# Nine places for expert weights, another order of the overflow passes, and a reordered router in a two-layer mixture-of-experts kernel

## What is computed

```python
def hierarchical_moe(h, w_rg, b_rg, w_re, b_re, w_gate, w_up, w_down):
    # 4 groups of 8 experts; a token takes the best group and its two best experts
    g_logits = t @ w_rg + b_rg
    g_sel = argmax(g_logits); g_p = softmax(g_logits)[g_sel]
    e_prob = softmax((t @ w_re + b_re)[g_sel])
    top_p, top_i = top_k(e_prob, 2)
    gates = g_p * top_p / sum(top_p)
    # for each of the 32 experts, over the tokens that chose it:
    hid = silu(xb @ w_gate[e]) * (xb @ w_up[e])      # hidden width 256
    y = hid @ w_down[e]
    # out[token] = sum of its two experts' y, each times its gate
```

## Time and profile before

| | us |
|---|---|
| median of 3 runs | 2986.21 (2985.51 to 2987.89) |
| the profiled execution, its own time | 2986.71 |
| its span, first to last instruction | 2985.0 |

### The profile page before, as it was taken

The page is one execution under the profiler, slowest core; times in us unless marked ns, Lnnn a source line. Parts: engine busy times, 40 slices in busy tenths (PEclk is TensorE's granted clock), DMA queues, the critical chain, the costliest instruction groups (busy, mean ns, idle before and its releaser), DMA issues.

```text
span 2985.0 us, 31524 instructions
## 1 busy us (share of the span) xinstructions
PE 2913.9 (98%) x12296; PEld 1856.9 (62%) x12296; DVE 1364.1 (46%) x2249; ACT 609.1 (20%) x1039; POOL 922.8 (31%) x729
## 2 busy tenths in 40 slices
PE   9999999999999999999999999999999999999998
PEld 7865464333468754643333588888664445888887
DVE  6733543333436435432444554442574464644442
ACT  2035323000210263230001400001212351300000
POOL 5500031554124110225551154443220102254442
PEclk9999999999999999999999999999999999999999
DMA  5211125999612201249998222222221111222220
GB/s 192 85 71 43 43 92 186 391 388 393 249 71 87 83 29 57 71 155 370 375 379 328 85 85 85 85 95 88 97 80 57 62 52 57 82 88 85 85 99 29
DMA packets 84165, 412.72 MB, mean 138 GB/s; under 512 B 27572, under 2 KB 30048, under 8 KB 37552
## 3 DMA queue, kind: packets, MB, share of 16 engines
q1 hardware_dynamic: 57664, 387.57, 34.2%
q0 software_dynamic: 26352, 23.12, 2.4%
HBM read 513.31 MB, written 31.46 MB: 183 GB/s over the span
## 4 chain that ended last, share of the span: by engine, by line
PE 89%; DVE 4%; DMA 4%; issue 1%; ACT 1%; SPq 0%; POOL 0%; DVEq 0%; ACTq 0%; POOLq 0%
PE PS L1139 38%; PE PS L1071 9%; PE PS L631 8%; PE PS L1093 5%; PE PS L616 4%; PE PS L709 4%; PE PS L589 4%; PE PS L1312 4%; DMA ring<-in_experts_gu 3%; PE PS L864 1%; PE PS L548 1%; PE PS L804 1%; PE PS L921 1%; PE PS L930 1%; PE PS L1379 1%
## 5 line engine op out<-in xcount | busy, mean ns | idle before, releaser
L3167 POOL TENSOR_TENSOR ATT<-ring 128x512 f32<-128x512 f32 (+1 forms) x97 | 126.3, 1302 | 1178.9 <-PE PS L1139 624.6
L1139 PE MATMUL PS<-G,ATT 128*128 128x256 f32 x1344 | 317.8, 379 | 0.0
L1139 PE MATMUL PS<-HT,ring 128*128 128x256 f32 x1376 | 313.8, 379 | 0.8 <-DVE BIG L1541 0.8
L1139 PE MATMUL PS<-G,ring 128*128 128x256 f32 x1216 | 287.6, 379 | 0.0
L1139 PEld LDWEIGHTS PS<-HT,ring 128*128 128x128 f32 x1376 | 261.2, 190 | 39.5 <-issue 2.4
L1139 PEld LDWEIGHTS PS<-G,ATT 128*128 128x128 f32 x1344 | 255.4, 190 | 36.0 <-issue 1.2
L631 PE MATMUL PS<-HT,ring 128*128 128x512 f32 x576 | 263.3, 600 | 0.0
L1139 PEld LDWEIGHTS PS<-G,ring 128*128 128x128 f32 x1216 | 231.0, 190 | 31.4
L2880 ACT ACTIVATE TMP<-PS 128x256 f32<-128x256 f32 x91 | 35.0, 384 | 1049.0 <-PE PS L1139 931.8
L1071 PE MATMUL PS<-ring,G 128*64 128x512 f32 x1024 | 228.8, 596 | 9.5 <-DMA ring<-in_experts_gu 9.0
L631 PEld LDWEIGHTS PS<-HT,ring 128*128 128x128 f32 x576 | 104.5, 190 | 127.4 <-issue 120.9
(11 more groups left out here) (387 smaller groups left out, 4315.2 us busy)
## 6 DMA issues: line engine op xcount, KB each, us to landing
ring<-in_stream SPq DMA_DIRECT2D x163, 1024.0 KB, 4.8
ring<-in_experts_gu SPq DMA_DIRECT2D x128, 1024.0 KB, 9.8
ring<-in_experts_down SPq DMA_DIRECT2D x64, 1024.0 KB, 8.8
G<-expert_rows SPq DMA_DIRECT2D x8, 1024.0 KB, 7.5
h_tokens<-G POOLq DMA_DIRECT2D x2, 2048.0 KB, 7.6
G<-h_tokens,ATT POOLq DMA_INDIRECT x156, 7.0
XT<-in_xT SPq DMA_DIRECT2D x1, 1024.0 KB, 8.3
G<-in_pT POOLq DMA_DIRECT2D x2, 512.0 KB, 6.4
```

Of the source, the lines that this page charges most:

```text
L1139: mm = pe.matmul(product(g, name), x[:, k * P:(k + 1) * P], y[:, k, :], start=first and k == 0 and name in opening, stop=last and k == h - ...
L3167: pool.tensor_tensor(a["S1"], a["A21"], a["A22"], ALU.add)\
```

## The change

- A main block's units go through nine places (`PLACE`): the six of the ring, two in `BIG` slots 16 to 23, one in `ATT` 7S to 11S. `experts()` hands them out in turn. SyncE loads the first nine units ahead: the two in `BIG` and five in the ring from the moment that the branches are done, the one in `ATT` and the last of the ring after the output projection and the projection tiles.
- To make room, the overflow weights have two places per side instead of three. Half 0 of gate-up and the down weights of one overflow block share a place, half 1 has the other, and the next overflow block has them the other way round (`tail_place`). So `tail_down` can be issued only when half 0 of the same block has been used, and half 1 of the next block only when this block's down is done. Gate-up comes as two pairs of DMAs instead of one pair.
- Overflow blocks stand behind every second main block, and at the end behind the 13th and the 15th: main 0, 1, tail 0, main 2, 3, tail 1, ... main 10, 11, tail 5, main 12, tail 6, main 13, 14, tail 7, main 15.
- Router: TensorE turns the logits first, then all token rows, counts the ranks, and only then works on the eight projection tiles. VectorE works out the gates (L1898 to L1909) behind L1970, and the overflow row numbers behind the gathers' row numbers. The zeroing of `BIG` goes, only `TMPF` is zeroed. The token rows are stored in two parts.

```diff
@@ block_order
-        if m % 2 == 0:
-            order.append(("tail", m // 2))
+        if m % 2 == 1 and m < PAIRS - 4 or m in (PAIRS - 4, PAIRS - 2):
+            order.append(("tail", tails))
+            tails += 1
@@ Ring
+            def experts(self):
+                order = [(self.place + i) % RING if i < RING else i for i in range(PLACES)]
+                for n in range(6 * PAIRS):
+                    p = order[n % PLACES]
+                    self.fills[p] += 1
+                    yield p, self.fills[p]
@@ places
-        TW = BIGF[:, 0:12 * D].rearrange("p (s n) -> p s n", s=2)
+        TW = BIGF[:, 0:8 * D].rearrange("p (s n) -> p s n", s=2)
+        PLACE = ([ring[:, i, :] for i in range(RING)] + [BIGF[:, (16 + 4 * i) * S:(20 + 4 * i) * S] for i in range(2)]
+                 + [ATT[:, 7 * S:11 * S]])
+        def tail_place(n, side, j):
+            i = (n + j) % 2
+            return TW[:, side, i * UNIT:(i + 1) * UNIT]
@@ TensorE, router
-                token_rows(0)
                 logits()
-                token_rows(1)
-                layer_tile(0)
-                token_rows(2)
-                layer_tile(1)
-                token_rows(3)
+                for t in range(TT):
+                    token_rows(t)
                 ranks()
-                for m in range(2, KD):
+                for m in range(KD):
                     layer_tile(m)
@@ TensorE, weights of a block
-                        if j == 0:
-                            pe.wait_ge(Q["tail_gu_landed"], now.next("tail_gu_landed", 32))
-                        if j == 2:
-                            pe.wait_ge(Q["tail_down_landed"], now.next("tail_down_landed", 32))
+                        landed = ("tail_gu_landed0", "tail_gu_landed1", "tail_down_landed")[j]
+                        pe.wait_ge(Q[landed], now.next(landed, 32))
@@ ScalarE, router
-                for i in range(2):
-                    act.activation(BIGF[:, i * 4 * S:(i + 1) * 4 * S], ONES[:, 0:1].to_broadcast([P, 4 * S]),
-                                   ACT.Identity, scale=0.0).then_inc(Q["rx_zeroed"], now.inc("rx_zeroed"))
-                act.activation(TMPF, ONES[:, 0:1].to_broadcast([P, D]), ACT.Identity, scale=0.0)\
-                    .then_inc(Q["rx_zeroed"], now.inc("rx_zeroed"))
@@ GpSimd, before the blocks
-                pool.memset(BIGF[:, 8 * S:], 0.0).then_inc(Q["tails_zeroed"], now.inc("tails_zeroed"))
-                pool.wait_ge(Q["lin_free"], at[f"htok{L}"])
-                pool.dma_start(HDR.rearrange("(t p) d -> p t d", p=P), HTOK).then_inc(Q["h_stored"], 16)
+                pool.wait_ge(Q["tile_done"], 2 * (at[f"out{L}"][1] + 3))
+                pool.memset(TMPF, 0.0).then_inc(Q["rows_zeroed"], now.inc("rows_zeroed"))
+                for t in range(0, TT, 2):
+                    pool.wait_ge(Q["lin_free"], at[f"htok{L}"] - 2 * (TT - 2 - t))
+                    pool.dma_start(HDR.rearrange("(t p) d -> p t d", p=P)[:, t:t + 2, :], HTOK[:, t:t + 2, :])\
+                        .then_inc(Q["h_stored"], 16)
@@ GpSimd, the loop over blocks
-                    if 1 <= q < NSEQ and ORDER[q - 1][0] == "tail" and ORDER[q - 1][1] + 1 < TAILS:
-                        pool.wait_ge(Q["gu_ready"], 2 * (L * NSEQ + q))
-                        tail_gate_up(L, ORDER[q - 1][1] + 1)
+                    if 1 <= q < NSEQ and ORDER[q - 1][0] == "tail":
+                        pool.wait_ge(Q["gu_ready"], 2 * (L * NSEQ + q) - 1)
+                        tail_down(L, ORDER[q - 1][1])
                     if q >= 2:
                         pool.wait_ge(Q["y_ready"], y0 + q - 1)
                         scatter(q - 2)
-                        kind, n = ORDER[q - 2]
-                        if kind == "tail" and n + 1 < TAILS:
-                            tail_down(L, n + 1)
+                    if 1 <= q < NSEQ and ORDER[q - 1][0] == "tail" and ORDER[q - 1][1] + 1 < TAILS:
+                        pool.wait_ge(Q["gu_ready"], 2 * (L * NSEQ + q))
+                        tail_gate_up(L, ORDER[q - 1][1] + 1, 0)
+                    if q >= 2 and ORDER[q - 2][0] == "tail" and ORDER[q - 2][1] + 1 < TAILS:
+                        pool.wait_ge(Q["dn_ready"], L * NSEQ + q - 1)
+                        tail_gate_up(L, ORDER[q - 2][1] + 1, 1)
@@ SyncE, loads of a layer's expert weights (after the change)
+                sp.wait_ge(Q["lin_ready"], at[f"branches{L}"])
+                weights(RING)
+                weights(RING + 1)
+                for n in range(RING - 1):
+                    weights(n)
+                sp.wait_ge(Q["unit_done"], at[f"out{L}_end"])
+                sp.wait_ge(Q["lin_ready"], at[f"projected{L}"])
+                weights(RING + 2)
+                weights(RING - 1)
+                for n in range(PLACES, len(units)):
+                    weights(n)
```

More of the change, by code:

```diff
@@ L28 @@
 RING = 6
+PLACES = 9
 EPS = 1e-6
@@ L1042, in two_units @@
                     if ORDER[q][0] == "tail":
-                        if j == 0:
-                            pe.wait_ge(Q["tail_gu_landed"], now.next("tail_gu_landed", 32))
-                        if j == 2:
-                            pe.wait_ge(Q["tail_down_landed"], now.next("tail_down_landed", 32))
-                        return [TW[:, side, j * UNIT:(j + 1) * UNIT] for side in range(2)], []
+                        landed = ("tail_gu_landed0", "tail_gu_landed1", "tail_down_landed")[j]
+                        pe.wait_ge(Q[landed], now.next(landed, 32))
+                        return [tail_place(ORDER[q][1], side, j) for side in range(2)], []
                     ws, units = [], []
                     for side in range(2):
-                        ws.append(unit())
-                        units.append(st["unit"])
+                        place, fill = next(places)
+                        pe.wait_ge(w_landed[place], 16 * fill)
+                        ws.append(PLACE[place])
+                        units.append((place, fill))
                     return ws, units
@@ L1103, in moe @@
                 at[f"moe{L}_y"] = now.count("y_ready")
+                places = plan.experts()
                 turn_x(0)
@@ L1119, in moe @@
                 down(NSEQ - 1)
+                assert next(places, None) is None
                 pe.wait_ge(Q["y_ready"], now.next("y_ready"))
@@ L3307, in experts, with weights @@
                     steps += [(q, 0), (q, 1)] + ([(q - 1, 2)] if q else [])
-                for q, j in steps + [(NSEQ - 1, 2)]:
-                    kind, m = ORDER[q]
-                    if kind == "main":
-                        for side in range(2):
-                            e = 2 * m + side
-                            load(A["experts_gu"][L, e, :, j, :] if j < 2 else A["experts_down"][L, e, :, :])
+                units = [(2 * ORDER[q][1] + side, j) for q, j in steps + [(NSEQ - 1, 2)] if ORDER[q][0] == "main"
+                         for side in range(2)]
+                places = list(plan.experts())
+                def weights(n):
+                    place, fill = places[n]
+                    if fill > 1:
+                        name, value = used[(place, fill - 1)]
+                        sp.wait_ge(Q[name], value)
+                    e, j = units[n]
+                    sp.dma_start(PLACE[place], A["experts_gu"][L, e, :, j, :] if j < 2 else A["experts_down"][L, e, :, :])\
+                        .then_inc(w_landed[place], 16)
+                sp.wait_ge(Q["lin_ready"], at[f"branches{L}"])
[9 more added lines that the diff above has]
+                    weights(n)
             for L in range(LAYERS):
```

123 lines of the change are left out of this document (65 added, 58 removed).

## The result

The changed kernel takes 3001.24 us (median of 5 runs, 2994.72 to 3002.83) against 2986.21: a ratio of 1.0046 with a 95% interval of 1.0035 to 1.0058. It is slower by 15 us where 10 less was forecast, and it lies 2 us above the range. Of the four cases, C (GpSimd's queue backs up, 3007) comes nearest. The profile is of the execution that took 2994.72, so it holds 8 of the 15 us (2993.0 against 2985.0 of span).

The account below looks back on a forecast made before the run. PE, busy 98% of the span, was taken as the bound, with only idle time to win. Ring -31.9, router -9.4, overflow waits +9, +3 and +18 gave -11.3 us: 2976 us against 2986.71 profiled, range 2952 to 2999.

Parts of the forecast that it names:

- C: Rival: GpSimd's queue backs up behind saturated weights, overflow DMAs land late; +21 us, 3007 us; chance 0.20.
- half 1 of the next overflow block: Expert stages: second gate-up pair, issued behind the scatter, lands slightly late; ten cases of 0.3 us, +3 us (0 to 15).
- the router: Router stage, both layers: logits first and ranks, slot table and gathers earlier; -9.4 us (bounds -6 and -10).
- The ring: Expert stages: nine places remove all of PE's stalls for ring weights in both layers; -31.9 us.
- the overflow passes' other two terms: Waits for overflow down weights, +9 us (0 to 34), and for gate-up ahead of tail 6, +18 us (9 to 22).
- What bounds the kernel: Whole kernel: PE, busy 98%, sets the time; only its idle time can be won, mainly waits for expert weights.
- PE has five projection tiles (about 1 us each) under VectorE's chain: Router: projection matmuls cover VectorE's chain, three more tiles under the gather; losing that cover would cost 3 us.
- the wait of 2.66 us for the logits: Router: L1835's wait behind eight turns; logits going first were to win 1.6 us of it (bounds 0 and 2.66).
- `tail_down`: Overflow blocks: down weights, issued behind four gathers, land 0.7 us late, 0.9 with restart; ten times, +9 us (0 to 34).
- 14.9 us after `down`: Overflow blocks: landing of the next block's second gate-up pair, needed after 14.7 us; 0.3 us wait each.
- the bound of 15: Upper bound, in us, of the half 1 waits, since two new DMAs ahead of the gathers fill GpSimd's queue; +3 taken.
- Tail 6: Overflow block two blocks behind the previous one: PE waits 9.0 us per layer for half 1; +18 us (9 to 22).

Follow-up runs that it names:

- the even order: Changed kernel with the overflow blocks behind main 0, 2, 4 ... 14 as before, none two blocks behind another: 3004.16 us, ratio 1.0056.
- seven places: Changed kernel with seven weight places instead of nine and the old overflow places and DMAs (four per overflow block), block order and router as changed: 2964.19 us, ratio 0.9925.
- the loads in halves: Changed kernel with each 1 MB load of expert weights issued as two DMAs of 64 partitions: 3303.85 us, ratio 1.1063.

## Why the prediction was wrong

Two terms of the sum failed: the waits for half 1 of the next overflow block, put at +3 us and 16.6 in the profiled execution, and the router, put at -9.4 and -4.9 measured. The ring and the overflow passes' other two terms came out near their values.

**What bounds the kernel, and the ring term.** Right. -31.9 us were forecast; without overflow DMAs 35 us are won (2950.84 against 2986.21), of which 3 to 5 are the router's, and layer 0 takes the 266.4 us of an unstalled stage.

**The router.** Right in sign, half in size: 4.9 us instead of 9.4. The failed step is "PE has five projection tiles (about 1 us each) under VectorE's chain". The five lie between the ranks and the slot table, and take over 1.7 us each; three more follow, and the first blocks' rows are turned only then, at 483.89. The timeline of layer 0 after the change:

```profile
467.44 8.83 PE L1011 MATMUL PS<-G,ring 128*128 128x512 f32 x20
476.10 1.90 PE L1028 MATMUL PS<-ATT 128*128 128x72 f32 x16
477.84 5.36 PE L1011 MATMUL PS<-G,ring 128*128 128x512 f32 x12
```

The slot table starts at 476.10 with no wait ahead of it, where 475.15 was forecast. The cover had become the path. The step rested on no row, where the timeline of before has one, eight of these matmuls, two tiles. A second step failed in layer 1, where only 1.6 of the forecast 4.7 us came: the wait of 2.66 us for the logits is layer 0's, and layer 1 had 1.60, which is 1.1 of the 3.1 us that are missing there:

```profile
471.35 3.68 PE L992 MATMUL PS<-G,ring 128*128 128x512 f32 x8
...
1297.98 0.31 DVE L1835 TENSOR_TENSOR ATT<-PS,RTOK 128x144 f32<-128x144 f32 x1 [1.60 <-PE PS L972]
```

**`tail_down`.** Right in size. The issue came when forecast, and for the landing, sized at 7.6 us behind four gathers, 7.65, 7.76 and 9.55 us were measured where it is in the chain of layer 0. Waits were fewer and longer than "ten times" 0.9 us: 2.7, 1.9, 1.3 and 0.3 us in layer 0 and 0.6 in layer 1, 8.0 us with the restarts, against 9.

**Half 1.** This is the term that failed most. "14.9 us after `down`" was set against a need after 14.7, so nearly no wait, "Ten such cases, 0.3 us each: +3". The profiled execution has seven, of 0.6, 1.6 and 1.7 us in layer 0 and 0.6, 2.2, 5.3 and 2.0 in layer 1: 13.9 us, and 16.6 with restarts and the low clock behind one, more than the bound of 15. (There are twelve cases, not ten: tail 7 also stands three blocks behind the one ahead of it, and it is two of the seven.) Landing times of 10 to 14.7 us stand in the chain where 10.1 was taken. The trace of before had them already. It has 24 `tail_down` DMAs beside a full weights queue, of which the earlier trace rows is two; the landing times of all (540 to 750 us, then 1380 to 1610 us):

```profile
DMA to landing us min/median/max: 8.5/9.9/11.3
...
DMA to landing us min/median/max: 8.7/10.3/14.5
```

At 14.5 us the same sum gives a wait of 4.6. So one pair was taken for the whole, in a step whose margin was 0.2 us. The bound of 15 us stood there with its reason, "the two new DMAs ahead of the gathers fill GpSimd's queue", and was then given almost no weight: it should have moved the value, as it was the mechanism of rival C.

**Tail 6.** The size is right by luck, its make-up isn't. Forecast were 9.0 us in each layer for half 1. The timeline has these two rows:

```profile
707.38 9.02 PE L1086 MATMUL PS<-BIG,G 128*64 128x512 f32 x32 [4.62 <-DMA BIG<-in_experts_gu,ATT]
...
1556.15 9.25 PE L1086 MATMUL PS<-BIG,G 128*64 128x512 f32 x32 [9.29 <-DMA BIG<-in_experts_gu,ATT]
```

That is 4.6 us and 9.3 us, ahead of half 0 (its pair is issued at 697.88 behind the down pair, gathers and a scatter), with 2.0 and 2.2 us behind them for the low clock: 18.1 us together, in whose cover half 1 lands. Taking tail 6 out of its place doesn't win them while the queue is full: in the even order as much is lost at other blocks.

**The clock.** Not in the sum: some 5.5 us in the profiled execution, which stand in the figures of half 1 and tail 6 above. Added up, the waits and what is behind them are 8.0 for `tail_down`, 16.6 for half 1 and 18.1 for tail 6, 42.7 of the 44.9 us; the forecast had 9, 3 and 18. With 4.5 us less from the router that explains the profiled execution. The median lies 6.5 us above it.

**The common failure** is that each wait was sized from the landing of one pair of DMAs, in a queue where latency isn't a constant, and that two more DMAs per overflow block were given no price. Beside a full weights queue 19 DMAs for three blocks passed without a wait for them (the kernel before; seven places) and 21 did not, in whatever order (2989.99 us at best, else 2999.34 to 3008.88), and the DMAs that are then late are those that stand last: down pairs, gate-up pairs, or gathers. The prediction counted bytes (1.05 MB) and packets, and never the number of DMAs.

The Trainium skill's rule that the prediction weighed ("DMA: Bandwidth & Descriptors", Queues, rings and completion order: DMA engines change between queues after a whole packet of many descriptors) would fit a price per DMA, if each small DMA waits for a turn of its own behind a packet of the weights queue, and if what the profile counts as packets are its descriptors. It agrees that cutting the profile's count from 144 to 48 per DMA brought nothing (3003.59 us). But no run here shows that rule at work; the loads in halves were meant to and settled nothing.

**Left open.** Whether the price, 23 to 36 us for 32 DMAs, lies in the queue's own handling or in the DMA engines. In the changed kernel 100 us of layer 0 (560 to 660) stand at a DMA share of 1.01 and 390 GB/s, against 1.02 and 403 with seven places, which speaks for the engines; with a quarter of the packets it is 0.94 and 369, and gathers are late all the same, which speaks for the queue. Nor is it known where between 19 and 21 it begins. The changed kernel's other runs lie up to 8 us above the profiled one, and no trace shows those.

## What to carry to other kernels

Count the DMAs of GpSimd's queue for a period of the work, empty ones too, before splitting one into two: beside a full weights queue two more in 32.5 us cost 0.7 us each in one kernel (23 us for 32) and 1.1 in another (36), in whatever wait stands last. Before a landing time goes into a sum, read all landings of its kind from the trace, and take the long ones where the margin is small. More places for prefetch pay only as long as they don't take the places by which some other transfer could be issued early; here one place more than six (2964.19 us) beats three more (3001.24). And work that hides a chain must be timed by its own rows, since a shorter chain makes it the path.

## What the runs showed of the hardware

- An indirect DMA that moves nothing has 144 packets and landed after 3.4 us beside a nearly idle weights queue and after 7.7 to 14.7 beside a full one (8.5 to 14.5 for 24 of them in the kernel before). 32 of them, added, cost 36 us and 23 us in two kernels; 2.7 us of GpSimd's time at each place cost 5 us in all.
- Loads of 64 partitions by 8 KB ran at 223 to 255 GB/s with a DMA share of 1.03 to 1.05, where loads of 128 partitions reach 400 to 409 at 1.01 to 1.02. The share of busy time doesn't tell them apart.
- Waits of PE of 4.6 to 9.3 us lowered its granted clock to 0.86, 0.72 and 0.52 in the stretch, and 16 matmuls behind one took 5.25 and 5.40 us instead of 3.51. The length of the wait alone doesn't decide: in the even order 16 matmuls took 5.35 us behind a wait of 2.24 us and 3.65 behind one of 2.28, and in the profiled executions of the kernel before and of the one with seven places no wait of the expert stages, 2.4 us at most, had such slow matmuls behind it.
